# A stage's first weight block multiplied tile by tile, low weights first, from turned tiles that lie in PSUM banks of their own

## The chip, the cores and the metric

One Trainium2 chip, one of its cores. The metric is the device time of the program in microseconds, median of several executions. Engines by the names of the profile: PE (TensorE matmuls), PEld (its weight loads), DVE (VectorE), ACT (ScalarE), POOL (GpSimd), SP (SyncE, which issues the weight transfers).

## What is computed

Two transformer blocks, one behind the other, on 256 tokens with 1024 features, all in float32. The first has a mixer (gated MLP, forgetting attention, attention to a memory) and a feed-forward layer with squared ReLU; the second has two layers, each a half-weighted SwiGLU, an attention (sliding window in layer 0, latent in layer 1) and another SwiGLU. Every part begins with a normalisation of x:

```python
def rmsnorm(x, g):
    xf = x.astype(jnp.float32)
    y = xf * lax.rsqrt(jnp.mean(jnp.square(xf), axis=-1, keepdims=True) + RMS_EPS)
    return (y * g.astype(jnp.float32)).astype(x.dtype)
...
        h = rmsnorm(x, norm_pre_ffn[l])
        f = jnp.square(jax.nn.relu(h @ w_ff1[l])) @ w_ff2[l]
        x = x + rmsnorm(f, norm_post_ffn[l])
...
def swiglu(h, wg, wu, wd):
    return (jax.nn.silu(h @ wg) * (h @ wu)) @ wd
...
    for i in range(DEPTH_2):
        x = x + 0.5 * swiglu(rmsnorm_2(x, ffn_norm1[i]), ffn1_wg[i], ffn1_wu[i], ffn1_wd[i])
        h = rmsnorm_2(x, mix_norm[i])
```

## The kernel before

**Stages.** The program runs M1, F0, F1, MA, F2, F3, MB, F4: the mixer of the first block, its feed-forward layer (F0, "relu"), and then two layers of SwiGLU (F1, F3), attention (MA, MB) and SwiGLU (F2, F4). x lies in SBUF as two token tiles of 128 (`t`), 1024 features wide.

**Products.** Precision comes from pairs: every weight and every activation is held as an upper part rounded to fp32r (`w_hi`, `h_hi`) and a lower part that is left (`w_lo`, `h_lo`). A product is hi x hi, hi x lo and lo x hi. `h_both` holds both parts of h side by side, so `wide_features_out` (L282) takes hi weights against 512 columns (both parts, `of_hi`, L288) and lo weights against 256 (`of_lo`, L292); `sum_halves` (L317) adds the two halves of the bank. `tokens_out` has the tokens as stationary side and makes three products of 256 or fewer columns (L262 to L264).

**Weights.** A list of blocks (mostly 128 x 2048) is loaded by SP through a ring of six raw slots. For every block ScalarE rounds (`round_block`, L231) and VectorE subtracts (`split_block`, L238), into a ring of three; `hi_ready`, `lo_ready` and `block_used` count blocks.

**A turn.** Between two stages, x must be transposed and normalised. This happens nine times, n = 0 (the memory), 1, and 2 to 8, where n = 2 stands before F0, 3 before F1, 4 before MA, 5 before F2, 6 before F3, 7 before MB and 8 before F4. I call them turns. From n = 2 on:

- TensorE: `plain_tensor_turn` (L437) transposes 8 tiles of 128 features for each token tile, when `x_ready` says that the half of x is there. Feature tiles 2j and 2j+1 share a bank. `keep_busy` (L258) are filler products on constants, ahead, amid and behind the transposes by `TURN_IDLE`; two of them (four passes of the array) stand behind at every turn.
- ScalarE: `norm_scalar_round` (L504) scales the eight tiles with the gain and rounds them into `h_hi`, for each pair of tiles when the pair is transposed, and then takes the squares of the second token tile (L377), for the scale 1/rms.
- VectorE: `norm_vector_split` (L513) makes `h_lo`, for each pair when ScalarE has done the pair. Then it splits one weight block, in most turns makes two diagonal matrices of the scale (`row_vector_diag`), splits another block and copies the row of scales (`row_vector_copy`). At n = 7 it waits for the second scale before it splits the first of these blocks.
- GpSimd: `rsqrt_pool` (L388, L389) turns the sum of squares into the scale.
- TensorE again: the first block of the stage is called with `wait_h` and waits for `h_lo_ready` pair by pair. In the F stages it takes the first 128 output features with hi and lo in turn, then the second 128 with all hi and then all lo. Then `row_tensor` (L475) spreads the scales over the partitions, and the second block follows.

The scale is applied later, to the sums, so that products need not wait for it. In MA the first block (256 columns) is `a_in`, in MB it is the first of `b_in` (160 columns), both by `tokens_out`.

**What sets the order.** Each engine runs its own list, written out by hand, in order. Semaphores tie the lists together. No scheduler moves anything.

Of the kernel before, what the change touches and what calls it, by code (L numbers as in the profile page):

```python
# [6 lines left out]
F32 = mybir.dt.float32  # L7
F32R = mybir.dt.float32r
I32 = mybir.dt.int32
ALU = mybir.AluOpType  # L10
# [20 lines left out]
def build(nc, i, out):  # L31
# [80 lines left out]
    with ExitStack() as ctx:  # L112
# [143 lines left out]
        def keep_busy(bank, count):  # L256
            for _ in range(count):
                nc.tensor.matmul(ps[:, bank, 0:TOK], ident[:, :], tri[:, 0:TOK], start=True, stop=True, skip_group_check=True)  # L258
# [10 lines left out]
        def features_out(b, to, turn=0, wait_h=None, of=tokens):  # L269
# [12 lines left out]
        def wide_features_out(b, bank, turn=0, wait_h=None):  # L282
# [4 lines left out]
            def of_hi(f, k):  # L287
                nc.tensor.matmul(ps[:, bank + f, :], hi[:, k, f * P:(f + 1) * P], h_both[:, k, :, :].rearrange("p a b -> p (a b)"),  # L288
                                 start=k == 0, stop=False, skip_group_check=True)

            def of_lo(f, k):
                return nc.tensor.matmul(ps[:, bank + f, 0:TOK], lo[:, k, f * P:(f + 1) * P], h_both[:, k, 0, :],  # L292
                                        start=False, stop=k == KD - 1, skip_group_check=True)

            if wait_h is not None:
                nc.tensor.wait_ge(lo_ready, b + 1 + RAW * turn)
                for k in range(KD):
                    if k % 2 == 0:
                        nc.tensor.wait_ge(h_lo_ready, wait_h + k // 2 + 1)
                    of_hi(0, k)  # L300
                    of_lo(0, k)
# [4 lines left out]
            for k in range(KD):  # L306
                of_hi(1, k)
            if wait_h is None:
# [3 lines left out]
            for k in range(KD):  # L312
                last = of_lo(1, k)
# [6 lines left out]
        def tokens_out(b, to, turn=0, wait_h=None, h0=0, wait_k=None, half_done=None, before=None, half_count=1, of=tokens):  # L320
# [5 lines left out]
            for t in order:  # L326
                if before and t == order[1]:
                    before()
                for c in range(0, cols, 512):
                    w = min(512, cols - c)  # L330
                    for k in range(k_n):
                        if wait_h is not None and t == order[0] and c == 0 and k % 2 == 0:
                            nc.tensor.wait_ge(h_lo_ready, wait_h + k // 2 + 1)
# [8 lines left out]
        def tokens_half(b, half, bank, wait_h=None):  # L342
# [4 lines left out]
            for t in range(TT):  # L347
                for k in range(k_n):
                    h = k_n * half + k
                    if wait_h is not None and t == 0:  # L350
                        nc.tensor.wait_ge(h_lo_ready, wait_h + h // 2 + 1)
# [10 lines left out]
        def turn_bank(n):  # L362
            return 2 if n in (2, 5, 8) else 0
# [43 lines left out]
        def norm_vector_diag(n):  # L407
            for t in range(TT):
                c = 2 * n + t
                nc.vector.wait_ge(norm_rstd, c + 1)  # L410
                if t == 0:
                    if n:
                        nc.vector.wait_ge(h_psum, 4 * n)
# [4 lines left out]
        def norm_tensor_turn(n, source):  # L418
            for t in range(TT):
                nc.tensor.wait_ge(diag_ready, 2 * n + t + 1)  # L420
                for k in range(KD):
                    col = (k % 2) * TOK + t * P
# [1923 lines left out]
```

## Time and profile before

| | us |
|---|---|
| median of 3 runs | 1248.69 |
| lowest and highest | 1248.62, 1248.9 |
| span of the profiled execution, first to last instruction | 1246.7 |
| what lies around the span (median less span) | 2.0 |

| engine | busy us | share of the span |
|---|---|---|
| PE | 1219.2 | 98% |
| PEld (beside PE) | 1045.0 | 84% |
| DVE | 897.9 | 72% |
| ACT | 617.3 | 50% |
| POOL | 127.7 | 10% |

Read it so: TensorE has work nearly all the time, and the shares of the others are averages over stages. At a turn, though, a short chain runs through all engines, and there TensorE may wait, or be filled with products that nobody needs. Filler counts as busy in the first table. So the turns have to be read in the timeline, engine by engine, with the time at which each operation starts.

### The profile page before, as it was taken

The page shows a single profiled execution, that of the slowest core. Times are in us where ns is not written, and L with a number is a line of the kernel's source. Part 1 is how long each engine was busy: PE and PEld are TensorE (multiplying, and loading weights), DVE is VectorE, ACT ScalarE, POOL GpSimd, SP SyncE. Part 2 cuts the span into 40 slices and gives each one's busy share as a digit, 9 for nine tenths or more (in the row PEclk, how much of TensorE's full clock was granted, in tenths as well). Part 3 has the DMA queues.
Part 4 walks back from the last instruction along what each step waited for, and adds up shares of the span by engine and source line. Part 5 has one row for each costly group of instructions (what it writes and reads, how often), then busy time and mean ns, then how long its engine had stood idle before and what let it go on. Part 6 is the DMA issues. An engine that isn't in the chain of part 4 may idle for free.

```text
span 1246.7 us, 17409 instructions
## 1 busy us (share of the span) xinstructions
PE 1219.2 (98%) x6798; PEld 1045.0 (84%) x6798; DVE 897.9 (72%) x1088; ACT 617.3 (50%) x795; POOL 127.7 (10%) x169
## 2 busy tenths in 40 slices
PE   7999999999999999989999999999999989999998
PEld 7996788888888888967888888888888877888887
DVE  5976777667967777675877776877676775877675
ACT  6765444444643444685534444544434795534442
POOL 4420300000400000340000000100000430000000
PEclk9999999999999999999999999999999999999999
DMA  9882595556565656443555555656554414556530
GB/s 309 252 238 98 123 263 194 182 201 202 180 210 188 200 179 194 167 133 102 182 190 200 180 193 169 198 182 201 185 176 149 135 35 135 186 186 201 180 123 34
DMA packets 156039, 219.36 MB, mean 176 GB/s; under 512 B 6104, under 2 KB 134172, under 8 KB 155852
## 3 DMA queue, kind: packets, MB, share of 16 engines
q1 hardware_dynamic: 153612, 212.28, 52.8%
q0 software_dynamic: 2368, 6.26, 2.1%
q8 instruction: 40, 0.66, 0.2%
q14 instruction: 19, 0.16, 0.0%
HBM read 213.26 MB, written 5.27 MB: 175 GB/s over the span
## 4 chain that ended last, share of the span: by engine, by line
PE 90%; DVE 5%; ACT 3%; issue 1%; POOL 1%; DMA 0%; SPq 0%; DVEq 0%; ACTq 0%; POOLq 0%
PE ps L288 30%; PE ps L292 15%; PE ps L262 13%; PE ps L263 13%; PE ps L264 13%; PE ps L677 1%; PE ps L702 1%; PE ps L690 1%; ACT h_both L504 1%; DVE w_lo L238 1%; DVE arena L782 1%; ACT w_hi L231 0%; DMA raw<-in_w_mem_kv 0%; DVE h_both L513 0%; PE ps L449 0%
## 5 line engine op out<-in xcount | busy, mean ns | idle before, releaser
L231 ACT CAST w_hi<-raw 128x2048 fp32r<-128x2048 f32 (+3 forms) x198 | 375.5, 1899 | 399.2 <-PE ps L292 270.3
L238 DVE TENSOR_TENSOR w_lo<-raw,w_hi 128x2048 fp32r<-128x2048 f32 (+3 forms) x197 | 449.6, 2284 | 152.6 <-ACT w_hi L231 150.5
L288 PE MATMUL ps<-h_both,w_hi 128*128 128x512 f32 x1664 | 402.3, 391 | 1.4 <-DVE h_both L513 1.4
L288 PEld LDWEIGHTS ps<-h_both,w_hi 128*128 128x128 f32 x1664 | 308.8, 188 | 66.6 <-issue 3.2
L292 PEld LDWEIGHTS ps<-h_both,w_lo 128*128 128x128 f32 x1664 | 216.1, 191 | 8.1
L292 PE MATMUL ps<-h_both,w_lo 128*128 128x256 f32 x1664 | 222.2, 283 | 0.0
L262 PE MATMUL ps<-w_hi,act_hi 128*128 128x512 f32 x500 | 195.9, 392 | 1.1 <-DVE act_lo L1985 0.7
L263 PE MATMUL ps<-w_lo,act_hi 128*128 128x512 f32 x500 | 195.2, 390 | 0.0
L264 PE MATMUL ps<-w_hi,act_lo 128*128 128x512 f32 x500 | 194.5, 389 | 0.0
L317 DVE TENSOR_REDUCE arena<-ps 128x512 f32<-128x1024 f32 x104 | 127.3, 1224 | 81.4 <-PE ps L292 80.7
L262 PEld LDWEIGHTS ps<-w_hi,act_hi 128*128 128x128 f32 x500 | 94.1, 188 | 20.7 <-DVE act_lo L1985 1.1
L264 PEld LDWEIGHTS ps<-w_hi,act_lo 128*128 128x128 f32 x500 | 93.9, 188 | 20.0
L263 PEld LDWEIGHTS ps<-w_lo,act_hi 128*128 128x128 f32 x500 | 94.1, 188 | 17.2
L388 POOL TENSOR_SCALAR rstd<-sums 128x1 f32<-128x1 f32 (+1 forms) x22 | 20.8, 944 | 828.1 <-ACT scratch L377 648.9
L1178 ACT CAST act_hi<-act 128x512 fp32r<-128x512 f32 x60 | 37.4, 624 | 113.5 <-DVE act L1256 99.6
L262 PE MATMUL ps<-w_hi,h_both 128*128 128x512 f32 (+4 forms) x256 | 87.6, 342 | 1.4 <-DVE h_both L513 0.8
L263 PE MATMUL ps<-w_lo,h_both 128*128 128x512 f32 (+4 forms) x256 | 85.3, 333 | 0.0
L264 PE MATMUL ps<-w_hi,h_both 128*128 128x512 f32 (+4 forms) x256 | 85.1, 333 | 0.0
L262 PEld LDWEIGHTS ps<-w_hi,h_both 128*128 128x128 f32 x256 | 48.4, 189 | 8.9 <-issue 4.2
L264 PEld LDWEIGHTS ps<-w_hi,h_both 128*128 128x128 f32 x256 | 48.5, 189 | 4.0
L263 PEld LDWEIGHTS ps<-w_lo,h_both 128*128 128x128 f32 x256 | 48.5, 189 | 3.4
L484 DVE TENSOR_TENSOR arena<-arena,row 128x512 f32<-128x512 f32 x60 | 41.5, 692 | 2.1
(252 smaller groups left out, 1055.7 us busy)
## 6 DMA issues: line engine op xcount, KB each, us to landing
raw<-in_ffn_wg SPq DMA_DIRECT2D x44, 1024.0 KB, 5.3
raw<-in_ffn_wu SPq DMA_DIRECT2D x44, 1024.0 KB, 5.3
raw<-in_ffn_wd SPq DMA_DIRECT2D x44, 1024.0 KB, 4.9
raw<-in_w_ff SPq DMA_DIRECT2D x32, 1024.0 KB, 5.4
raw<-in_a_w_in SPq DMA_DIRECT2D x5, 1024.0 KB, 5.3
raw<-in_w_in SPq DMA_DIRECT2D x4, 1024.0 KB, 7.5
raw<-in_w_out SPq DMA_DIRECT2D x4, 1024.0 KB, 7.0
raw<-in_a_w_out SPq DMA_DIRECT2D x4, 1024.0 KB, 5.0
```

What stands on the lines that cost most here:

```text
L231: nc.scalar.copy(w_hi[:, place(b), 0:n], raw[:, b % RAW, 0:n]).then_inc(hi_ready, 1)
L238: nc.vector.tensor_tensor(w_lo[:, place(b), 0:n], raw[:, b % RAW, 0:n], w_hi[:, place(b), 0:n].bitcast(F32), ALU.subtract).then_inc(lo_rea ...
L262: nc.tensor.matmul(to, still[0], moving[0], start=start, stop=False, skip_group_check=True)
L263: nc.tensor.matmul(to, still[0], moving[1], start=False, stop=False, skip_group_check=True)
L264: return nc.tensor.matmul(to, still[1], moving[0], start=False, stop=stop, skip_group_check=True)
L288: nc.tensor.matmul(ps[:, bank + f, :], hi[:, k, f * P:(f + 1) * P], h_both[:, k, :, :].rearrange("p a b -> p (a b)"), start=k == 0, stop=F ...
L292: return nc.tensor.matmul(ps[:, bank + f, 0:TOK], lo[:, k, f * P:(f + 1) * P], h_both[:, k, 0, :], start=False, stop=k == KD - 1, skip_gro ...
L317: return nc.vector.tensor_reduce(to.rearrange("p (f t) -> p f t", f=2), ps[:, bank:bank + 2, :].rearrange("p f (h t) -> p f t h", h=2), AX ...
L388: pool_then(nc.gpsimd.tensor_scalar(to, sums_of, 1.0 / count, eps, ALU.mult, ALU.add))
L484: return nc.vector.tensor_tensor(to.rearrange("p (f t) -> p f t", f=2), source.rearrange("p (f t) -> p f t", f=2), row_of_both, ALU.mult)
L504: last = nc.scalar.activation(norm_home(n, k)[0], ps[:, turn_bank(n) + j, half * TOK:(half + 1) * TOK], ACT.Copy, scale=norm_gain(n, k))
L1178: nc.scalar.copy(act_hi[:, buf, :], act[:, buf, :]).then_inc(hidden_hi[st], 1)
```

## The change

1. **Banks.** For n = 2 to 8 the turned tiles 0 to 5 lie in six banks, one each, in the first half of the bank; tiles 6 and 7 lie in the second halves of the banks of tiles 4 and 5. Turns 0 and 1 stay as they were. Semaphores count tiles and not pairs. ScalarE takes a tile when it is turned (tiles 4 and 5 when 6 and 7 are turned too), and tiles 6 and 7 only when VectorE is through with 4 and 5. VectorE takes each tile when ScalarE has done it.
2. **Order of the first block.** For every feature tile k: lo weights x upper tokens for both halves of the output, as soon as `h_hi` of tile k is there; then hi weights x both parts for tile k-1, when `h_lo` of k-1 is there. In MA and MB a new function, `tokens_out_first`, does the same with the upper tokens as stationary side.
3. **Filler.** The two `keep_busy` products behind the transposes go, at all seven turns. Those ahead and amid keep their number and write to the second half of a bank.
4. **Row products.** `row_tensor` moves from behind the first block into the middle of the second (`amid`), between the hi products of its two halves.
5. **Bank moves that follow.** The first gate block of F1 and F3 goes to banks 6 and 7, the `a_in` blocks start at bank 6 (`a_bank`), the first two of MB at 6 and 5; two of the later transposes in MA swap banks and one waits for one more `a_squares`.

```diff
         def wide_features_out(b, bank, turn=0, wait_h=None, amid=None):
...
             if wait_h is not None:
+
                 nc.tensor.wait_ge(lo_ready, b + 1 + RAW * turn)
-                for k in range(KD):
-                    if k % 2 == 0:
-                        nc.tensor.wait_ge(h_lo_ready, wait_h + k // 2 + 1)
-                    of_hi(0, k)
-                    of_lo(0, k)
+                for k in range(KD + 1):
+                    if k < KD:
+                        nc.tensor.wait_ge(h_hi_ready, wait_h + k + 1)
+                        for f in range(2):
+                            of_lo(f, k)
+                    if k:
+                        nc.tensor.wait_ge(h_lo_ready, wait_h + k)
+                        for f in range(2):
+                            last = of_hi(f, k - 1)
...
-        def turn_bank(n):
-            return 2 if n in (2, 5, 8) else 0
+        def turned(n, k):
+
+            if n < 2:
+                bank, half = k // 2, k % 2
+            else:
+                bank, half = (2 if n in (2, 5, 8) else 0) + (k if k < 6 else k - 2), k // 6
+            return ps[:, bank, half * TOK:(half + 1) * TOK]
...
-        TURN_IDLE = {2: (0, 3, 2), 3: (1, 2, 2)}
+        TURN_IDLE = {2: (0, 3), 3: (1, 2)}
...
-            keep_busy(left, behind)
...
         def norm_scalar_round(n):
...
+            for k in range(KD):
+                nc.scalar.wait_ge(h_psum, 8 * n + (k + 2 - k % 2 if n < 2 else k + 3 if k in (4, 5) else k + 1))
+                if n >= 2 and k >= 6:
+                    nc.scalar.wait_ge(h_lo_ready, 8 * n + k - 1)
+                nc.scalar.activation(norm_home(n, k)[0], turned(n, k), ACT.Copy, scale=norm_gain(n, k)).then_inc(h_hi_ready, 1)
...
         def norm_vector_split(n):
...
+            for k in range(KD):
+                nc.vector.wait_ge(h_hi_ready, 8 * n + (k + 2 - k % 2 if n < 2 else k + 1))
...
         def swiglu_tensor(st, n, s, turn=0):
...
-            wide_features_out(b_gate(st, s), 0, turn=turn, wait_h=4 * n if s == 0 else None)
-            if s == 0:
-                row_tensor(n)
+            wide_features_out(b_gate(st, s), gate_bank(st, s), turn=turn, wait_h=8 * n if s == 0 else None)
...
-            wide_features_out(b_upper(st, s), 2, turn=turn)
+            wide_features_out(b_upper(st, s), 2, turn=turn, amid=(lambda: row_tensor(n)) if s == 0 else None)
```

The new function of MA and MB, with its main part:

```python
        def tokens_out_first(b, bank, wait_h):
...
            for k in range(KD + 1):
                if k < KD:
                    nc.tensor.wait_ge(h_hi_ready, wait_h + k + 1)
                    for t in range(TT):
                        still = h_hi[:, k, t * P:(t + 1) * P]
                        nc.tensor.matmul(to(t), still, hi[:, k, :], start=k == 0 and t == 0, stop=False, skip_group_check=True)
                        nc.tensor.matmul(to(t), still, lo[:, k, :], start=False, stop=False, skip_group_check=True)
                if k:
                    nc.tensor.wait_ge(h_lo_ready, wait_h + k)
                    for t in range(TT):
                        last = nc.tensor.matmul(to(t), h_lo[:, k - 1, t * P:(t + 1) * P], hi[:, k - 1, :],
                                                start=False, stop=k == KD, skip_group_check=True)
```

TensorE at turn 3, from the last transposes into the first block of F1, before the change (`ident,x` are transposes, `tri,ident` filler, `w_hi` and `w_lo` the halves of the weights):

```order
L449 MATMUL ps<-ident,x 128x128 x3
L258 MATMUL ps<-tri,ident 128x256 x2
L288 MATMUL ps<-h_both,w_hi 128x512 [waits h_lo_ready,lo_ready]
L292 MATMUL ps<-h_both,w_lo 128x256
L288 MATMUL ps<-h_both,w_hi 128x512
L292 MATMUL ps<-h_both,w_lo 128x256
L288 MATMUL ps<-h_both,w_hi 128x512 [waits h_lo_ready]
```

The same place with the change:

```order
L480 MATMUL ps<-ident,x 128x128 x3
L292 MATMUL ps<-h_both,w_lo 128x256 [waits h_hi_ready,lo_ready]
L292 MATMUL ps<-h_both,w_lo 128x256
L292 MATMUL ps<-h_both,w_lo 128x256 [waits h_hi_ready]
L292 MATMUL ps<-h_both,w_lo 128x256
L288 MATMUL ps<-h_both,w_hi 128x512 [waits h_lo_ready]
L288 MATMUL ps<-h_both,w_hi 128x512
L292 MATMUL ps<-h_both,w_lo 128x256 [waits h_hi_ready]
```

The filler is gone, four lo products stand ahead of the first hi product, and the first wait is for the upper part of one tile, not for the lower part of two.

ScalarE at turn 2, from x's first to its second tile of squares (L377), before the change:

```order
L504 ACTIVATE h_both<-ps,gain_col 128x256 [waits h_psum]
L504 ACTIVATE h_both<-ps,gain_col 128x256
L504 ACTIVATE h_both<-ps,gain_col 128x256 [waits h_psum]
L504 ACTIVATE h_both<-ps,gain_col 128x256
L377 ACTIVATE scratch,sums<-x 128x1024 [waits y_sumsq,sumsq_ready,x_ready]
```

The same place with the change (the squares are now L410):

```order
L534 ACTIVATE h_both<-ps,gain_col 128x256 [waits h_psum] x6
L534 ACTIVATE h_both<-ps,gain_col 128x256 [waits h_lo_ready,h_psum] x2
L410 ACTIVATE scratch,sums<-x 128x1024 [waits y_sumsq,sumsq_ready,x_ready]
```

The list is the same, but the last two tiles, and with them the squares, now stand behind VectorE (`h_lo_ready`).

## Rows read from the trace of the kernel before

**Rows 1.** The page: busy time and share of TensorE; the chain by engine.
```profile
PE 1219.2 (98%) x6798; PEld 1045.0 (84%) x6798; DVE 897.9 (72%) x1088; ACT 617.3 (50%) x795; POOL 127.7 (10%) x169
...
PE 90%; DVE 5%; ACT 3%; issue 1%; POOL 1%; DMA 0%; SPq 0%; DVEq 0%; ACTq 0%; POOLq 0%
```

**Rows 2.** Timeline of TensorE at turn 3: start us, us, engine, line, operation.
```profile
320.29 1.03 PE L258 MATMUL ps<-tri,ident 128*128 128x256 f32 x4
...
321.50 0.47 PE L288 MATMUL ps<-h_both,w_hi 128*128 128x512 f32 x1 [0.19 <-DVE h_both L513]
...
321.81 0.28 PE L292 MATMUL ps<-h_both,w_lo 128*128 128x256 f32 x1
...
324.57 2.01 PE L288 MATMUL ps<-h_both,w_hi 128*128 128x512 f32 x8
...
327.37 0.61 PE L475 MATMUL ps<-diag,tri 128*128 128x128 f32 x4
...
331.48 2.08 PE L292 MATMUL ps<-h_both,w_lo 128*128 128x256 f32 x16
...
333.39 3.82 PE L288 MATMUL ps<-h_both,w_hi 128*128 128x512 f32 x16
```

**Rows 3.** Timeline at turn 3 of ScalarE, VectorE and GpSimd.
```profile
319.61 3.05 ACT L504 ACTIVATE h_both<-ps,gain_col 128x256 fp32r<-128x256 f32 x8 [1.31 <-PE ps L449]
...
320.48 3.22 DVE L513 SCALAR_TENSOR_TENSOR h_both<-ps,gain_col,h_both 128x256 fp32r<-128x256 f32 x8 [0.74 <-ACT h_both L504]
...
323.78 2.18 POOL L388 TENSOR_SCALAR rstd<-sums 128x1 f32<-128x1 f32 x1 [3.63 <-ACT scratch L377]
...
329.54 1.22 DVE L317 TENSOR_REDUCE arena<-ps 128x512 f32<-128x1024 f32 x1
```

**Rows 4.** Timeline of TensorE at turn 6.
```profile
777.78 1.03 PE L258 MATMUL ps<-tri,ident 128*128 128x256 f32 x4
...
785.08 0.61 PE L475 MATMUL ps<-diag,tri 128*128 128x128 f32 x4
```

**Rows 5.** Timeline of TensorE and VectorE at turn 4.
```profile
506.35 1.03 PE L258 MATMUL ps<-tri,ident 128*128 128x256 f32 x4
...
509.91 4.48 DVE L238 TENSOR_TENSOR w_lo<-raw,w_hi 128x2048 fp32r<-128x2048 f32 x2
...
513.74 0.28 PE L262 MATMUL ps<-w_hi,h_both 128*128 128x256 f32 x1
```

**Rows 6.** Timeline at turn 2 of TensorE, VectorE and GpSimd.
```profile
139.91 2.28 DVE L238 TENSOR_TENSOR w_lo<-raw,w_hi 128x2048 fp32r<-128x2048 f32 x1
...
140.07 2.17 POOL L388 TENSOR_SCALAR rstd<-sums 128x1 f32<-128x1 f32 x1 [3.63 <-ACT scratch L377]
...
142.91 0.15 DVE L468 TENSOR_SCALAR y_scale<-rstd 128x1 f32<-128x1 f32 x1 [0.46 <-POOL rstd L389]
...
149.19 0.69 DVE L1182 TENSOR_TENSOR act_lo<-act,act_hi 128x512 fp32r<-128x512 f32 x1 [0.69 <-ACT act_hi L1178]
...
149.98 0.47 PE L262 MATMUL ps<-w_hi,act_hi 128*128 128x512 f32 x1
```

**Rows 7.** Timeline at turn 7 of TensorE, VectorE and GpSimd.
```profile
964.06 1.03 PE L258 MATMUL ps<-tri,ident 128*128 128x256 f32 x4
...
967.77 0.19 POOL L388 TENSOR_SCALAR rstd<-sums 128x1 f32<-128x1 f32 x1 [4.46 <-ACT scratch L377]
...
968.62 4.49 DVE L238 TENSOR_TENSOR w_lo<-raw,w_hi 128x2048 fp32r<-128x2048 f32 x2 [0.92 <-POOL rstd L389]
...
971.18 0.32 PE L262 MATMUL ps<-w_hi,h_both 128*128 128x256 f32 x1
```

**Rows 8.** Waits of TensorE: for whom, us in total, times, longest us.
```profile
PE ps L677 <- DVE small L782: 5.7, 9, 1.2
```

**Rows 9.** Groups of instructions: line, operation, count; busy us, mean ns; idle.
```profile
L423 PE MATMUL ps<-diag,arena 128*128 128x128 f32 x32 | 5.7, 359 | 0.0
...
L423 PE MATMUL ps<-diag,x 128*128 128x128 f32 x32 | 3.7, 275 | 0.0
```

More of the change, by code:

```diff
@@ L305, in wide_features_out @@
                     of_hi(0, k)
-            for k in range(KD):
-                of_hi(1, k)
-            if wait_h is None:
+                if amid:
+                    amid()
+                for k in range(KD):
+                    of_hi(1, k)
                 nc.tensor.wait_ge(lo_ready, b + 1 + RAW * turn)
@@ L311, in wide_features_out @@
                     of_lo(0, k)
-            for k in range(KD):
-                last = of_lo(1, k)
+                for k in range(KD):
+                    last = of_lo(1, k)
             last.then_inc(block_used, 1)
@@ L431, in x_halves @@
             return 4 * r + 2 * t + half + 1
-        TURN_IDLE = {2: (0, 3, 2), 3: (1, 2, 2)}
+        TURN_IDLE = {2: (0, 3), 3: (1, 2)}
         def plain_tensor_turn(n):
-            ahead, amid, behind = TURN_IDLE.get(n, (0, 0, 2))
-            left = y_bank(n - 2, 0) + 1
-            keep_busy(turn_bank(n) + 3, ahead)
+            ahead, amid = TURN_IDLE.get(n, (0, 0))
+            spare = 2 if n == 2 else 0
+            keep_busy(spare, ahead, TOK)
             for t in range(TT):
@@ L2070, in project @@
                     for half in halves_now:
-                        tokens_half(b + half, half, bank, wait_h=4 if p == 2 and half == 0 else None)
+                        tokens_half(b + half, half, bank, wait_h=8 if p == 2 and half == 0 else None)
                 elif features:
@@ L2202, in _ @@
                         tensor.wait_ge(a_squares, p - 3)
-                    tokens_out(first["a_in"] + p, lambda t, c, w: ps[:, 4 + p % 4, t * TOK + c:t * TOK + c + w],
-                               wait_h=16 if p == 0 else None, before=(lambda: scores_tensor(heads_a[0:2])) if p == 4 else None)
+                    if p == 0:
+                        tokens_out_first(first["a_in"], a_bank(0), 32)
+                        continue
+                    tokens_out(first["a_in"] + p, lambda t, c, w: ps[:, a_bank(p), t * TOK + c:t * TOK + c + w],
+                               before=(lambda: scores_tensor(heads_a[0:2])) if p == 4 else None)
                     if p >= 2:
@@ L2247, in turn_latent @@
                     last.then_inc(c_turned, 1)
-                tokens_out(first["b_in"], lambda t, c, w: ps[:, 4, t * TOK + c:t * TOK + c + w], wait_h=28)
+                tokens_out_first(first["b_in"], 6, 56)
                 b = first["b_in"] + 1
```

86 lines of the change are left out of this document (42 added, 44 removed).

## The prediction, made before the changed kernel ran

> **What bounds the kernel now.** The page's shares come first. TensorE is busy for 1219.2 of 1246.7 us and the chain that ended last is 90% PE [rows 1]: only what shortens TensorE's own line, or a hole in it, moves the end. The median of the runs, 1248.69, is the span and 2.0 us around it; I subtract from the span and add the 2.0 back.
>
> The change works at the seven turns n = 2 to 8, where a stage's x is transposed and its first weight block multiplied. I read TensorE's timeline at turn 3 [rows 2]. The last transpose is followed at 320.29 by the "behind" filler, the first product starts at 321.50, the second half's products run 324.57 to 327.37, and there the row products (L475) begin. From the end of the transposes to the end of the block it is 7.08 us. The work in it: the second half's eight hi products (512 columns) and eight lo products (256 columns) take 327.37 - 324.57 = 2.80 us, or 0.35 a pair, so 16 pairs make 5.6 us. A lo product alone takes (333.39 - 331.48) / 16 = 0.119 us, which leaves 0.231 for a hi product. So 1.47 us of the turn is filler, wait and pacing. The other engines show why [rows 3]: ScalarE rounds eight tiles in 3.05 us from 319.61 (0.36 us each), VectorE starts 0.87 later at 320.48, after two of them, and takes 3.22 (0.39 each). TensorE starts when VectorE's second tile is done, and then is held at VectorE's 0.39 us against its own 0.35 per tile.
>
> **The change, part by part.**
>
> *Order of the products, separate banks, filler gone.* No product is added or dropped. The new first block needs only the rounded upper tile to begin. ScalarE waits for one transpose, not two, so it starts about 0.1 earlier (one transpose cadence); its first tile is there about 0.5 later, near 320.05, before the transposes end at 320.29. VectorE now follows one tile behind ScalarE, not two: it starts near 320.0, its first lower tile is ready by about 320.65, with the 0.15 that a hand-over takes; TensorE asks for it after four lo products, at 320.29 + 0.48 = 320.77. From then TensorE uses 0.70 us a tile (two lo, two hi) against VectorE's 0.39, so it never waits again. It is its own bound: the block takes 5.6 us from 320.29 and ends at 325.9, against 327.37. Gain **1.47** at turn 3. The filler behind (four passes, 1.03 us) costs nothing now, since it covers the wait; once the wait is gone it would cost its whole 1.03, and its removal is part of this sum, not more. The fillers ahead and amid stay in number and only change bank: 0.
>
> Turns 5, 6 and 8 repeat the pattern. At turn 6 it is 777.78 to 785.08, or 7.30 [rows 4]; turns 5 and 8 have 7.19 and 7.17. There the transposes of both token tiles run together, so TensorE reaches the first lo product about 0.05 before its tile: 7.30 - 5.61 - 0.05 = **1.64** at turn 6, and about **1.57** each at 5 and 8.
>
> Turn 4 (a_in) has 48 products of 256 columns at 0.12: 5.76 us. Before, 506.35 to 513.74 is 7.39 [rows 5]. With 0.05 at the start: **1.58**. The next block then wants the lower part of its weights at 512.16. VectorE makes two splits of 2.24 from 509.91; moved 0.25 earlier (below), the first ends at 511.9. It is just met.
>
> *What is late next.* ScalarE's tiles 6 and 7 share a bank with 4 and 5 and wait until VectorE is through with them. ScalarE would start tile 6 at about +2.15 from its first, VectorE's tile 4 ends at 0.5 + 5 x 0.39 = +2.5: ScalarE ends 0.35 later than before, and with it the squares of x's second tile (L377). VectorE ends its eight tiles 0.25 earlier (0.5 earlier start, less what it waits for the late tiles 6 and 7). Two turns hang on these two numbers.
>
> Turn 2 (relu stage): TensorE's first second-product starts at 149.98, right behind the lower half of the hidden activations (149.19 + 0.69 = 149.88) [rows 6], so it already waits for VectorE there. Behind that lies one unbroken VectorE line from 139.91: split, POOL's rstd, diagonal, split, row, sum, scaling. In the new kernel TensorE comes 1.5 us early and stands. What counts is the VectorE line, and its only gap is the wait for POOL, released at 142.91. POOL's L388 starts at 140.07 and takes 2.17 us, ending with VectorE's split (139.91 + 2.28 = 142.19); at turn 7, with no split running, the same operation takes 0.19 [rows 6, 7]. So POOL ends with the split, which comes 0.25 earlier; squares 0.35 later still fall inside it. Gain **0.25**. The Trainium skill, "SBUF — State Buffer", section "SBUF: two separate sides", says that VectorE and GpSimd share a port pair as an exclusive lock held for the whole instruction; the trace agrees (2.17 against 0.19). If POOL did not stand, this turn's gain would be 0.25 and the 0.46 us of VectorE's wait, 0.7 in all.
>
> Turn 7 (b_in): the first block is 964.06 to 971.18 [rows 7]; its 48 products are narrower (160 columns), so they take at most turn 4's 5.76 us and, started at 964.06, would end by 969.8, at least 1.3 us sooner. But here VectorE waits for the second rstd before it splits the second block's weights: ScalarE's squares, POOL at 967.77, split 968.62 to 970.9. TensorE may enter the second block only then. With the squares 0.35 later the split ends near 971.25, against a start at 971.18 before: **-0.1**. The whole gain turns into a wait of 1.4 us or a little more.
>
> *Do turns 3, 5, 6, 8 keep theirs?* TensorE's next condition on VectorE is the sum of the first block: VectorE starts it at 329.54 and takes 1.22, TensorE needs it at 333.39 [rows 2, 3]. Slack 2.6, after the change 2.6 - 1.47 + 0.25 = 1.4. The row products move to the middle of the second block, where their diagonals are ready; in turn 3 they would otherwise be asked for at 325.9, before POOL has released them. They take the same 0.36 either way. Turns 3, 5, 6 and 8 keep the gain. After turn 4, ScalarE takes each a_in block out as TensorE ends it, so it comes earlier with TensorE, and the attention, whose waits (5.7 us for VectorE's L782 [rows 8]) lie among engines that all start earlier, shifts as a whole.
>
> *Bank moves* (gates of F1, F3 in banks 6 and 7, a_bank, b_in in 6; the stricter wait of the last a_in transpose): each waits on work that is over when it is asked for; 0. Waits that are met cost nothing: at 331.48 and 333.39 the cadence stays 0.119 and 0.23 [rows 2]. Turns 0 and 1 keep their order and banks: 0.
>
> Sum: 1.47 + 2 x 1.57 + 1.64 + 1.58 + 0.25 - 0.1 = 8.0 us. 1246.7 - 8.0 = 1238.7; with 2.0 around it, **1240.7**.
>
> **The rivals.**
> 1. VectorE's line binds in the swiglu stages as it does in turn 2. Then turns 3, 5, 6, 8 gain 0.25 each: 1.58 + 5 x 0.25 - 0.1 = 2.7, **1246.0**. It needs VectorE 1.4 us later than its rows say. Against it stands the slack above. 8 in 100.
> 2. The clock falls in the new holes (1.3 us at turn 2, 1.4 or more at turn 7, with no filler). The longest wait of the kind now is 1.2 us [rows 8], at a granted clock of 1.00. For a price, the kernel's first 32 turning products took 5.7 us against 3.7 for the next 32 [rows 9]: 2 us for each fall, both turns: **1244.7**. The Trainium skill, "TensorE: Matmul & The Clock Gate", section "What's actually happening", makes throttling the default that activity lifts; no run here shows a fall after so short a hole. 8 in 100.
> 3. Waits cost even when met: an unmet one makes the first product 0.31 instead of 0.23 (321.50 to its successor at 321.81 [rows 2]). 16 waits x 0.08 at five turns is 6.4 of the 8.0: **1247.1**, no change. The met waits above speak against it. 6 in 100.
> 4. Slower: squares decide everywhere. If POOL's rstd follows ScalarE's squares and not the split, and VectorE's line behind it binds at all turns, each turn loses the 0.35 by which tiles 6 and 7 delay the squares: 7 x 0.35 = 2.4, **1251.1**. It decides once rstd is later than the split's end and the slack of 1.4 is gone. At turn 3 POOL's L388 takes 2.18 us [rows 3], as at turn 2: it stands under a split there too, so the squares have room to come late. 4 in 100.
> 5. Turns 2 and 7 gain too, if the squares come early enough: up to 1.3 each, **1238.1**. 8 in 100.
>
> **How the numbers follow.** The forecast has 66 in 100. A range of 1238.0 to 1245.0 holds it with rivals 2 and 5, 82 in 100. A measurement of this kernel tells 0.2% from no change, 2.5 us: below 1246.2 lie the forecast and rivals 1, 2, 5: 0.90 faster; rival 3 0.06; rival 4 0.04.
>
> **What the changed profile would show.** At turns 3, 5, 6, 8 the lo products follow the transposes at once, and the second block starts 5.6 us after them. PE's idle grows at two places only: about 1.3 us before the first second-product of F0, 1.4 or more before b_in's second block. The squares (L377's successor) start 0.35 later after the first rounded tile. I am wrong if TensorE stands inside the new block, if its cadence in it is over 0.70 us a tile, or if new PE waits on gate_summed or the a_in weights appear.

## The result, and the profile after

| | before, us | after, us |
|---|---|---|
| median | 1248.76 (5 executions, 1248.62 to 1249.04) | 1241.65 (5 executions, 1241.56 to 1244.47) |
| ratio to before | 1 | 0.995, 95% interval 0.9939 to 0.9961 |
| span of the profiled execution | 1246.7 | 1242.1 |

The kernel is faster by 7.1 us. I had forecast 1240.7. But the five executions are not one group. Three lie at 1241.56 to 1241.65 with a granted TensorE clock of 1.000, two at 1244.45 and 1244.47 with 0.997. The profiled execution is one of the latter. That is a second finding beside the first, and it was one of the rivals. The median is the time of an undisturbed execution only because three of the five were undisturbed.

The page of the changed kernel: TensorE's busy time fell by 5.7 us, and the chain is TensorE for 92% of the span, where it was 90% [rows 1].

```profile
PE 1213.5 (98%) x6770; PEld 1042.9 (84%) x6770; DVE 897.5 (72%) x1088; ACT 616.6 (50%) x795; POOL 124.3 (10%) x169
...
PE 92%; DVE 4%; ACT 2%; issue 1%; DMA 0%; POOL 0%; SPq 0%; DVEq 0%; ACTq 0%; POOLq 0%
```

Turn 3 in TensorE's timeline (start us, us, engine, line, operation) answers [rows 2]:

```profile
320.59 1.32 PE L480 MATMUL ps<-ident,x 128*128 128x128 f32 x8 [0.47 <-DVE x L641]
321.66 0.72 PE L292 MATMUL ps<-h_both,w_lo 128*128 128x256 f32 x4
322.22 0.63 PE L288 MATMUL ps<-h_both,w_hi 128*128 128x512 f32 x2
322.69 0.40 PE L292 MATMUL ps<-h_both,w_lo 128*128 128x256 f32 x2
322.93 0.62 PE L288 MATMUL ps<-h_both,w_hi 128*128 128x512 f32 x2
...
326.41 2.91 PE L288 MATMUL ps<-h_both,w_hi 128*128 128x512 f32 x12
```

No wait is printed between the transposes and the end of the block. A tile's four products take 322.93 - 322.22 = 0.71 us, and the steps from tile to tile behind it are 0.69 or 0.70. Of the twelve hi products from 326.41 on, four still belong to this block and eight to the next.

Turn 2, rows of ScalarE, VectorE and TensorE (answers [rows 6]):

```profile
135.90 2.30 ACT L534 ACTIVATE h_both<-ps,gain_col 128x256 fp32r<-128x256 f32 x6 [1.08 <-PE ps L480]
...
138.86 0.84 ACT L534 ACTIVATE h_both<-ps,gain_col 128x256 fp32r<-128x256 f32 x2 [0.65 <-DVE h_both L540]
...
143.16 0.15 DVE L498 TENSOR_SCALAR y_scale<-rstd 128x1 f32<-128x1 f32 x1 [0.46 <-POOL rstd L422]
...
149.43 0.69 DVE L1211 TENSOR_TENSOR act_lo<-act,act_hi 128x512 fp32r<-128x512 f32 x1 [0.68 <-ACT act_hi L1207]
...
150.22 0.47 PE L262 MATMUL ps<-w_hi,act_hi 128*128 128x512 f32 x1 [1.76 <-issue]
...
152.04 0.63 PE L264 MATMUL ps<-w_hi,act_lo 128*128 128x512 f32 x1
...
154.41 0.40 PE L264 MATMUL ps<-w_hi,act_lo 128*128 128x512 f32 x1
```

Turn 7, rows of the same engines and of POOL (answers [rows 7]):

```profile
961.44 0.87 ACT L534 ACTIVATE h_both<-ps,gain_col 128x256 fp32r<-128x256 f32 x2 [0.35 <-DVE h_both L540]
...
963.43 0.19 POOL L421 TENSOR_SCALAR rstd<-sums 128x1 f32<-128x1 f32 x1 [4.83 <-ACT scratch L410]
...
964.29 4.49 DVE L238 TENSOR_TENSOR w_lo<-raw,w_hi 128x2048 fp32r<-128x2048 f32 x2 [1.46 <-POOL rstd L422]
...
966.63 0.58 PE L262 MATMUL ps<-w_hi,h_both 128*128 128x256 f32 x1 [1.67 <-DVE w_lo L238]
967.01 0.42 PE L263 MATMUL ps<-w_lo,h_both 128*128 128x256 f32 x1
...
970.11 0.28 PE L263 MATMUL ps<-w_lo,h_both 128*128 128x256 f32 x1
```

TensorE now stands for 1.76 us at turn 2 and 1.67 us at turn 7. At turn 2 the view names nobody for the wait (`issue`), but the hole ends just behind VectorE's `act_lo` (149.43 + 0.69 = 150.12). Behind the hole of turn 2 a matmul of 512 columns takes 0.63 us instead of 0.40 for some time (152.04 against 154.41), behind that of turn 7 one of 256 columns takes 0.42 instead of 0.28 (967.01 against 970.11). The windows behind the two holes show the granted clock (third number from the end, after the engines' busy times), first of the changed kernel:

```profile
150.00:154.00 4.00, 3.77 (x10) 3.04 (x11) 2.89 (x3) 1.20 (x1) 0.00 (x0) 0.59 1.04 178
966.00:970.00 4.00, 3.37 (x16) 3.37 (x17) 3.07 (x4) 3.06 (x9) 2.79 (x2) 0.57 0.55 167
```

and of the kernel before:

```profile
150.00:154.00 4.00, 4.00 (x18) 3.33 (x19) 3.00 (x2) 0.97 (x1) 0.00 (x0) 1.00 1.03 168
966.00:970.00 4.00, 4.00 (x36) 3.92 (x35) 3.08 (x6) 3.48 (x5) 0.74 (x2) 1.00 0.00 0
```

0.59 and 0.57 are mixtures of the two levels, 2.4 and 1.2 GHz. In the first window ten matmuls stand where eighteen stood.

To place the gain I took the start of the second token tile's first transpose at each turn from the timelines, and the stretches between them. e1 (below) is the changed kernel with both holes filled, an execution without a fall of the clock; lengths in us, gains against the kernel before.

| stretch | before | after (profiled) | e1 | gain forecast | gain in e1 |
|---|---|---|---|---|---|
| start to turn 2 | 135.42 | 135.54 | 135.65 | 0 | -0.23 |
| turn 2 to 3 | 183.72 | 185.05 | 183.80 | 0.25 | -0.08 |
| 3 to 4 | 186.34 | 184.85 | 184.85 | 1.47 | 1.49 |
| 4 to 5 | 85.14 | 83.53 | 83.50 | 1.58 | 1.64 |
| 5 to 6 | 186.29 | 184.75 | 184.77 | 1.57 | 1.52 |
| 6 to 7 | 186.28 | 184.76 | 184.75 | 1.64 | 1.53 |
| 7 to 8 | 94.67 | 96.37 | 94.88 | -0.1 | -0.21 |
| 8 to end | 188.80 | 187.28 | 187.30 | 1.57 | 1.50 |
| span | 1246.66 | 1242.12 | 1239.48 | 8.0 | 7.18 |

The five turns with a gain came in as priced. The two falls of the clock cost 185.05 - 183.80 = 1.25 us and 96.37 - 94.88 = 1.49 us.

### The profile page after: what moved, and what is told of

The parts are those of the page before. It is cut to its first block, busy times and chain, and to the rows that moved or that the text cites. A ratio compares the mean times of both kernels' runs of the same rounds, so it can differ in the third digit from the quotient of the medians.

```text
span 1242.1 us, 17367 instructions
## 1 busy us (share of the span) xinstructions
PE 1213.5 (98%) x6770; PEld 1042.9 (84%) x6770; DVE 897.5 (72%) x1088; ACT 616.6 (50%) x795; POOL 124.3 (10%) x169
## 4 chain that ended last, share of the span: by engine, by line
PE 92%; DVE 4%; ACT 2%; issue 1%; DMA 0%; POOL 0%; SPq 0%; DVEq 0%; ACTq 0%; POOLq 0%
PE ps L288 31%; PE ps L292 16%; PE ps L262 13%; PE ps L263 13%; PE ps L264 13%; PE ps L703 1%; PE ps L728 1%; PE ps L480 1%; PE ps L716 1%; DVE arena L808 1%; DMA raw<-in_w_mem_kv 0%; DVE w_lo L238 0%; PE ps L972 0%; PE ps L973 0%; PE ps L455 0%
## 5 line engine op out<-in xcount | busy, mean ns | idle before, releaser
L421 POOL TENSOR_SCALAR rstd<-sums 128x1 f32<-128x1 f32 (+1 forms) x22 | 17.3, 787 | 827.5 <-ACT scratch L410 647.8
L262 PE MATMUL ps<-w_hi,h_both 128*128 128x512 f32 (+3 forms) x224 | 79.0, 353 | 2.3 <-DVE w_lo L238 1.7
L263 PE MATMUL ps<-w_lo,h_both 128*128 128x512 f32 (+3 forms) x224 | 77.1, 344 | 0.0
L264 PE MATMUL ps<-w_hi,h_both 128*128 128x512 f32 (+3 forms) x224 | 76.8, 343 | 0.0
L262 PEld LDWEIGHTS ps<-w_hi,h_both 128*128 128x128 f32 x224 | 43.1, 192 | 9.0 <-issue 2.6
L264 PEld LDWEIGHTS ps<-w_hi,h_both 128*128 128x128 f32 x224 | 43.0, 192 | 4.0
L263 PEld LDWEIGHTS ps<-w_lo,h_both 128*128 128x128 f32 x224 | 43.1, 192 | 3.5
```

What stands on the lines that cost most here:

```text
L262: nc.tensor.matmul(to, still[0], moving[0], start=start, stop=False, skip_group_check=True)
L263: nc.tensor.matmul(to, still[0], moving[1], start=False, stop=False, skip_group_check=True)
L264: return nc.tensor.matmul(to, still[1], moving[0], start=False, stop=stop, skip_group_check=True)
L421: pool_then(nc.gpsimd.tensor_scalar(to, sums_of, 1.0 / count, eps, ALU.mult, ALU.add))
```

## The experiments

All were timed in five rounds beside the kernel before. e1 to e4 ran together, then e5 to e8 on another chip, then e9 with e10 on the chip of e1 to e4.

### e1: fill both holes

```diff
             if s == 1:
                 nc.tensor.wait_ge(row_ready, FEED[2] + 1)
+                keep_busy(7, 3)
...
                 tokens_out_first(first["b_in"], 6, 56)
+                keep_busy(7, 3)
```

> The changed kernel, with three filler products (about 1.5 us) put into each of the two holes that its trace shows: ahead of the first second-product of F0 (turn 2) and ahead of b_in's second block (turn 7). Nothing else is changed. Theory A: the executions of the changed kernel at 1244.5 are those in which the clock falls to its lower level after the two holes, those at 1241.6 the ones in which it does not; with the holes filled every execution is near 1241.6 and the granted clock is 1.000 in all, since the fillers end before what TensorE waits for is there. Rival B: the slow executions come from something else (for example weights that land late); then some executions stay at 1244.5. Rival C: the filler runs past the end of the hole and costs up to 0.3 us at each place: 1242.0 or so.

Measured: 1241.79 (1241.72 to 1241.84), granted clock 1.000 in all five. TensorE at the two places, and the window behind the first:

```profile
148.42 1.46 PE L258 MATMUL ps<-tri,ident 128*128 128x256 f32 x6
150.29 0.50 PE L262 MATMUL ps<-w_hi,act_hi 128*128 128x512 f32 x1 [0.41 <-DVE act_lo L1211]
...
963.63 1.50 PE L258 MATMUL ps<-tri,ident 128*128 128x256 f32 x6
965.47 0.39 PE L262 MATMUL ps<-w_hi,h_both 128*128 128x256 f32 x1 [0.34 <-DVE w_lo L238]
```

```profile
150.00:154.00 4.00, 3.71 (x16) 3.06 (x17) 2.89 (x3) 1.31 (x1) 0.00 (x0) 1.00 1.01 145
```

The filler ends 0.41 and 0.34 us before the data is there, so it costs nothing: with the hole of turn 2 open and no fall behind it (profile of e10, below) the stretch is 183.80 too, with that of turn 7 open (e2) it is 94.90 against 94.88. The clock stays at 2.4 GHz, and no execution lies near 1244.5. That fits theory A. Five executions alone wouldn't show it, since three of the five of the changed kernel had no fall either; the rows of the clock behind the holes speak for it, here and in e9.

### e2 and e10: fill one hole only

e2 has only the first of the two added lines of e1, e10 only the second.

> The changed kernel with filler in the hole of turn 2 only (ahead of the first second-product of F0), none at turn 7. Theory A: each hole makes its own fall of the clock, at a price of half of 2.9 us; executions lie at 1241.6 or, if the clock falls at turn 7, at 1243.0. Rival: one hole brings the fall at both places, then all are at 1241.6 or at 1244.5.

> The changed kernel with filler in the hole of turn 7 only, the hole of turn 2 (1.8 us) left open. Theory A: some executions 1.7 us above the rest, with the clock down from about 150.7 us on and at no other place of the two; the rest at 1241.8. Rival: only the hole of turn 7 matters, then all are at 1241.8.

Measured. e2: 1241.7, 1241.8, 1241.87 and 1241.97 at a clock of 1.000, 1243.6 at 0.999, 1245.08 at 0.997. e10: 1241.56, 1241.79, 1242.03 and 1242.03 at 1.000, 1242.91 at 0.999, 1243.72 at 0.998. Each kernel with one hole has slower executions, but not always. That the hole brings them isn't shown by these counts: beside e10 the kernel before had 3 of 11 executions below 1.000, beside e2 it had 1 of 18. The execution at 1245.08 is further off than one fall of 1.5 us explains. No slow execution of the two has a trace, so where their clock fell stays open. The profiled executions of both had no fall, behind open holes of 1.67 us (e2) and 1.76 us (e10).

### e3: the filler behind the transposes put back

```diff
+            keep_busy(BEHIND[n], 2, TOK)
+
+        BEHIND = {2: 0, 3: 6, 4: 7, 5: 0, 6: 6, 7: 7, 8: 0}
```

> The changed kernel with the two filler products behind the transposes put back at all seven turns (into a bank that is free there). Theory of the prediction: with the new order nothing covers them, so at turns 3, 4, 5, 6 and 8 each set costs its 0.9 to 1.0 us, and at turns 2 and 7 it only shortens the hole: 5 x 0.95 = 4.7 us above the undisturbed 1241.6, 1246.3. The holes of turns 2 and 7 are then 0.9 us shorter, and the clock stays up. Rival: the filler still lies beside a wait for the upper tiles and costs under 1 us in all: 1242.5.

Measured: 1245.44 (1245.27 to 1245.63), clock 1.000 in all six. Turn 3:

```profile
320.54 1.03 PE L258 MATMUL ps<-tri,ident 128*128 128x256 f32 x4
321.21 0.83 PE L292 MATMUL ps<-h_both,w_lo 128*128 128x256 f32 x4
321.88 0.62 PE L288 MATMUL ps<-h_both,w_hi 128*128 128x512 f32 x2
```

The stretches behind turns 3, 4, 5, 6 and 8 are longer than in e1 by 0.83, 0.73, 0.75, 0.68 and 0.74 us, together 3.7; the others are the same. So the filler is a cost once nothing lies beneath it. It is less than the 4.7 that I expected: the four passes cost their distance and not their length. The next product starts 0.67 us after the first of them (321.21 - 320.54), not 1.03, and the block's first product starts 0.62 to 0.76 us later than in e1. The holes of turns 2 and 7 are 0.93 us long here, not closed, and no execution had a fall.

### e4: the kernel before without that filler

```diff
-            keep_busy(left, behind)
```

> The kernel before with only the two filler products behind the transposes taken away, at all seven turns. Theory of the prediction: they cover a wait for VectorE's second tile, so their removal alone brings 0: 1248.7. Rival: they hold up the first product by the idle that the issue behind them takes (0.1 us each): 1248.0. Second rival: the holes of 1.2 us that they leave bring the clock down in some executions, 1.4 us each time.

Measured: 1249.04, ratio 1.0001 (0.9992 to 1.001). Eight of eleven executions lie at 1248.55 to 1249.14 with the clock at 1.000, three at 1250.46 to 1250.96 with 0.997 or 0.998. The profiled one is of the latter. TensorE at turn 3, and the window there:

```profile
321.62 0.49 PE L288 MATMUL ps<-h_both,w_hi 128*128 128x512 f32 x1 [1.05 <-DVE h_both L512]
...
322.12 0.63 PE L288 MATMUL ps<-h_both,w_hi 128*128 128x512 f32 x1
```

```profile
321.00:325.00 4.00, 3.38 (x11) 2.99 (x12) 4.00 (x9) 4.00 (x8) 1.12 (x1) 0.62 0.00 0
```

Under the old order the filler's time was free, as the prediction had it. Its removal alone brings 0 and leaves a hole at each of the seven turns, 1.05 to 1.28 us long. In this execution the clock fell behind one of the seven, that of turn 3 (1.05 us, one of the two shortest), and the stretch from turn 3 to 4 is 187.69 us instead of 186.34, 1.35 more. That the filler kept the clock up before the change is likely from this, but not shown: 3 of 11 executions against 1 of 18 of the kernel before beside it are too few to tell apart.

### e5: tiles 6 and 7 in the banks of 2 and 3

```diff
-                bank, half = (2 if n in (2, 5, 8) else 0) + (k if k < 6 else k - 2), k // 6
+                bank, half = (2 if n in (2, 5, 8) else 0) + (k if k < 6 else k - 4), k // 6
...
-                nc.scalar.wait_ge(h_psum, 8 * n + (k + 2 - k % 2 if n < 2 else k + 3 if k in (4, 5) else k + 1))
+                nc.scalar.wait_ge(h_psum, 8 * n + (k + 2 - k % 2 if n < 2 else k + 5 if k in (2, 3) else max(k + 1, 8 if k > 3 else 0)))
...
-                    nc.scalar.wait_ge(h_lo_ready, 8 * n + k - 1)
+                    nc.scalar.wait_ge(h_lo_ready, 8 * n + k - 3)
```

Both fillers of e1 are in it.

> The kernel of e1 (holes filled), with tiles 6 and 7 in the second halves of the banks of tiles 2 and 3 instead of 4 and 5. ScalarE then waits for VectorE's tiles 2 and 3, which are long done when it comes to 6 and 7. Theory: ScalarE's stop before tile 6 (2.97 us after the second token tile's first transpose, against 2.58 in the kernel before) is what delays the squares at turn 7 and VectorE's last tiles at turn 2. Without it ScalarE starts tile 6 at about 2.5, the squares at 3.3, VectorE is 0.4 earlier (0.6 at turn 2, where the stop was longer). Turn 7 gains 0.4, turn 2 0.6, the other turns nothing: 1240.8 against 1241.8. Rival: the split ahead of the rstd or POOL's wait under it decides, and nothing is gained: 1241.8.

Measured: 1240.71 (1240.39 to 1240.72), clock 1.000. ScalarE at turn 2, and VectorE at turn 7:

```profile
136.18 3.18 ACT L534 ACTIVATE h_both<-ps,gain_col 128x256 fp32r<-128x256 f32 x8 [1.08 <-PE ps L480]
```

```profile
962.28 4.50 DVE L238 TENSOR_TENSOR w_lo<-raw,w_hi 128x2048 fp32r<-128x2048 f32 x2 [1.27 <-POOL rstd L422]
```

The eight tiles are one run of 3.18 us again, where the changed kernel had six, a stop of 0.65 us and two. At turn 7 VectorE starts its splits 5.31 us after the second token tile's first transpose, where it was 5.81. The stretch from turn 2 to 3 is 183.29 (0.51 less than e1), that from 7 to 8 is 94.38 (0.50 less), all the others behind turn 2 are the same within 0.02 (turn 2 itself is reached 0.17 later). So the stop before tile 6, small as it is, reached the end of the kernel at exactly the two turns where the prediction had VectorE's line or the squares in charge.

### e6: at turn 7, split first and wait afterwards

```diff
+                split_block(late - 1)
                 if n == 7:
                     vector.wait_ge(norm_rstd, 2 * n + 2)
-                split_block(late - 1)
```

The filler of turn 2 is in it, that of turn 7 is not.

> The kernel of e2 (hole of turn 2 filled), and at turn 7 VectorE splits the weights of b_in's second block before it waits for the second rstd, not after. Theory: at turn 7 the new order's gain (1.6 us) is eaten by this wait alone; TensorE then enters the second block 0.2 to 0.3 us after the first instead of 1.8, POOL's operation stands under the split and the rstd comes 1.3 later, which ScalarE has room for: turn 7 to 8 is 1.5 shorter, 1240.3. Rival: the rest of MB (its rstds, its lower halves) waits for the later rstd, and the gain goes there: 1241.8 or above.

Measured: 1240.35 (four executions at 1240.25 to 1240.51, one of them with the clock at 0.999; one at 1242.42, also at 0.999). The last has no trace. In the profiled execution neither turn has a hole of more than 0.42 us, so slower executions come without these holes too. VectorE and POOL at turn 7:

```profile
961.49 2.28 DVE L238 TENSOR_TENSOR w_lo<-raw,w_hi 128x2048 fp32r<-128x2048 f32 x1
964.49 2.29 DVE L238 TENSOR_TENSOR w_lo<-raw,w_hi 128x2048 fp32r<-128x2048 f32 x1 [0.72 <-POOL rstd L422]
```

```profile
962.17 1.64 POOL L421 TENSOR_SCALAR rstd<-sums 128x1 f32<-128x1 f32 x1 [4.83 <-ACT scratch L410]
963.90 0.55 POOL L422 TENSOR_TENSOR rstd<-rstd,halves 128x1 f32<-128x1 f32 x1
```

The stretch from turn 7 to 8 is 93.55, 1.33 less than in e1: the turn's gain is there, and MB does not give it back. POOL's operation takes 1.64 us now, where it took 0.19 (963.43 in the changed kernel). It starts at 962.17, under the split, and ends with it (961.49 + 2.28 = 963.77). With squares that come at any time within the split, its end is the split's end.

### e7: the old order of the halves

```diff
-                for k in range(KD + 1):
-                    if k < KD:
-                        nc.tensor.wait_ge(h_hi_ready, wait_h + k + 1)
-                        for f in range(2):
-                            of_lo(f, k)
-                    if k:
-                        nc.tensor.wait_ge(h_lo_ready, wait_h + k)
-                        for f in range(2):
-                            last = of_hi(f, k - 1)
+                for k in range(KD):
+                    nc.tensor.wait_ge(h_lo_ready, wait_h + k + 1)
+                    of_lo(0, k)
+                    of_hi(0, k)
+                for k in range(KD):
+                    of_lo(1, k)
+                for k in range(KD):
+                    last = of_hi(1, k)
```

Both fillers of e1 are in it. Within each half the lo products now stand ahead of the hi products, which the kernel before had the other way round, and the wait is for one tile, not for two.

> The kernel of e1 with the F stages' first block in the old order of halves: half 0 with both weights tile by tile as the lower tile comes, then half 1 (MA and MB keep the new order; banks, semaphores per tile and the missing filler stay as in the changed kernel). Theory of the prediction: the order is worth about 1.0 us at each of turns 3, 5, 6, 8 (the block would start at the lower tile, 0.5 later, and be held to VectorE's 0.39 us a tile, 0.5 more), and nothing at turn 2: 1241.8 + 4 x 1.0 = 1245.8. The other 0.5 of each turn's 1.5 come from waiting for one tile instead of two. Rival: the separate banks and the semaphores per tile bring most of it: under 1243.

Measured: 1246.23 (1245.63 to 1246.63), clock 1.000. Turn 3:

```profile
321.35 0.35 PE L292 MATMUL ps<-h_both,w_lo 128*128 128x256 f32 x1 [0.19 <-DVE h_both L539]
321.55 0.39 PE L288 MATMUL ps<-h_both,w_hi 128*128 128x512 f32 x1
...
323.05 0.39 PE L288 MATMUL ps<-h_both,w_hi 128*128 128x512 f32 x1
...
323.44 0.40 PE L288 MATMUL ps<-h_both,w_hi 128*128 128x512 f32 x1
```

The block starts 1.50 us after the first transpose instead of 1.07, and its hi products then come at VectorE's 0.39 us (323.05 to 323.44). The stretches behind turns 3, 5, 6 and 8 are longer than in e1 by 0.94, 0.98, 1.00 and 0.97. Of the 1.5 us at such a turn, then, 1.0 is the order. The other 0.5 are what is left by subtraction: one tile waited for instead of two, and the filler gone, which no run separates.

Not expected were 0.42 us at turn 2, which I had priced at nothing. The trace has the reason:

```profile
145.45 0.60 PE L504 MATMUL ps<-diag,tri 128*128 128x128 f32 x4
...
146.09 0.42 DVE L509 COPY row<-ps 128x256 f32<-128x256 f32 x1 [0.31 <-PE ps L504]
```

TensorE is later with the first block, so the row products in the middle of the second (part 4 of the change) come at 145.45, where they came at 144.22 in e1. VectorE now waits 0.31 us for them, and it is VectorE's line that sets the time at this turn.

### e8: the three repairs together

> e2, e5 and e6 together: hole of turn 2 filled, tiles 6 and 7 in the banks of 2 and 3, the split first at turn 7. Theory: VectorE's split at turn 7 ends before TensorE has done the first block, so no hole is left there. Turn 2 gains 0.6, turn 7 up to 1.7: 1239.5. If MB waits for the later rstd: 1241.2.

Measured: 1239.46 (1239.3 to 1239.79), clock 1.000 in all five, ratio to the kernel before 0.9924 (0.991 to 0.9937). TensorE at turns 2 and 7:

```profile
148.28 1.46 PE L258 MATMUL ps<-tri,ident 128*128 128x256 f32 x6
149.66 0.50 PE L262 MATMUL ps<-w_hi,act_hi 128*128 128x512 f32 x1
...
962.51 0.61 PE L346 MATMUL ps<-w_hi,h_both 128*128 128x160 f32 x4
962.96 0.35 PE L262 MATMUL ps<-w_hi,h_both 128*128 128x256 f32 x1
```

At turn 7 the second block follows the first without a wait. The stretch from 7 to 8 is 93.24, 1.43 less than before the change; that from 2 to 3 is 183.27, 0.45 less. This is the fastest version here, and both new holes are gone. Older waits of TensorE stay in it as in every kernel here, one of 2.07 us near 13 us and one of 1.21 us near 102 us.

### e9: the changed kernel again

> The changed kernel as it is, for more executions beside the kernel before on one chip. Theory A (holes bring the clock down in some executions): again most executions at 1241.6 to 1241.9 with granted clock 1.000, and some of them 1.4 (0.999) or 2.9 us (0.997) above. Rival: the slow executions of the first measurement were chance as in the kernel before (1 of 23 there so far in these two sessions), then all lie at 1241.7.

Measured: 1243.25, 1243.3 and 1243.38 at a clock of 0.999, 1244.12 and 1244.51 at 0.997, 1247.22 at 0.995; not one execution at 1.000, where I had expected most at it. Ratio 0.9956 (0.9941 to 0.9971). Of the kernel before, three of eleven executions beside it had a clock below 1.000 as well (1251.02 to 1252.89), eight lay at 1248.7 to 1249.23.

The profiled execution (1244.12) has the two falls at the places where the first profile had them:

```profile
150.00:154.00 4.00, 3.88 (x11) 3.06 (x12) 2.88 (x3) 1.11 (x1) 0.00 (x0) 0.61 1.03 152
966.00:970.00 4.00, 3.47 (x16) 3.47 (x17) 3.07 (x4) 2.96 (x8) 2.79 (x2) 0.58 0.60 175
```

The stretches behind turns 2 and 7 are 185.06 and 96.39, against 183.80 and 94.88 in e1, and the others are as in e1. The execution at 1247.22 is 5.6 us above the undisturbed time, more than two falls cost, and it has no trace.

All executions, as they ran together; "low" are those with a clock below 1.000:

| ran together | kernel before | kernels with a new hole open | new holes filled, shortened or closed |
|---|---|---|---|
| the result | 0 of 5 low | changed kernel 2 of 5 | |
| e1 to e4 | 1 of 18 | e2 2 of 6, e4 3 of 11 | e1 0 of 5, e3 0 of 6 |
| e5 to e8 | 0 of 14 | | e5 0 of 5, e6 2 of 5, e7 0 of 10, e8 0 of 5 |
| e9 and e10 | 3 of 11 | changed kernel 6 of 6, e10 2 of 6 | |

The changed kernel, with both holes, is low in 8 of 11, the kernel before in 4 of 48, the kernels of the last column in 2 of 36. None of the last ran beside e9, when the kernel before had most of its low executions too. A clock of 0.999 is not always a slower execution: of the two of e6, one took 1240.25, as little as the rest. So the holes make falls more frequent; that filling them brings the falls back to the rate of the kernel before is what the counts suggest; that it rules them out isn't shown.

## Why the prediction was right, and where it was not

**The mechanism and its size: right.** The working of turn 3 (5.6 us of products, started at the end of the transposes) gave 1.47 and measured 1.49; turns 4, 5, 6 and 8 gave 1.58, 1.57, 1.64 and 1.57 and measured 1.64, 1.52, 1.53 and 1.50. e7 shows that the order is the larger part of it at turns 3, 5, 6 and 8: delay of the start and VectorE's pacing, 1.0 us of 1.5. Turn 4, and the remaining 0.5, no run takes apart. The slack of 1.4 us on VectorE's first sum was enough, since TensorE has no new wait in these stages. Rivals 1 and 4 are out, and so is rival 5: turns 2 and 7 gained nothing until e5 and e6.

**Filler free before, a cost after: right, over-priced.** e4 showed 0 before, e3 a cost after, of 0.68 to 0.83 us a turn instead of my 1.03. I had added the length of a pipelined group; its cost is the distance to the next start.

**Met waits cost nothing: right.** Four products a tile take 0.70 us, as worked out, with two waits among them. Rival 3 is out.

**Turn 7: right in kind.** The gain became a wait of 1.67 us. -0.21 measured against -0.1. e6 names the cause: with the split ahead of the wait, 1.33 us come back.

**Turn 2: wrong by 0.33.** The failed step is "VectorE ends its eight tiles 0.25 earlier". At turns 3 to 8 VectorE's last tile starts 0.17 earlier than before, but at turn 2 it starts 0.13 later (4.23 us after the transpose against 4.10), since ScalarE began tile 6 at 3.32 us instead of 2.64. At the other turns this was 2.97 to 3.02. The delay of the squares was mis-sized with it: 0.35 forecast, 0.43 at most turns, 0.70 at turn 2. e5 closes the stop and brings 0.5 at each of the two turns that hang on it. At turn 3 tile 6 starts 0.1 us after VectorE's fifth tile ends (2.92 and 3.02 us after the transpose), which is what it waits for; at turn 2 the fifth ends at 2.93 too, but tile 6 starts only at 3.32, as the sixth ends. Why, with the same code, stays open. That POOL's rstd ends with the split, so that late squares do no harm of their own, held: in the changed kernel VectorE still waits 0.46 for it (143.16), as in [rows 6].

**Start-up: 0.23 of the difference in e1.** Turn 2 is reached at 135.42 in the kernel before and at 135.44 to 135.82 in the others. The text there is not changed in its order, and I read nothing into it.

**The clock: right as a mechanism, wrong in its chance.** Rival 2 had 8 in 100. One fall or both came in 8 of 11 executions of the changed kernel. The median of e9 was 1243.75, nearer to the 1244.7 of the rival than to the forecast, and it was luck that the median of the first five executions was one without a fall. The step that failed is the evidence against the rival. I had read one row, a longest wait of 1.2 us at a clock of 1.00 [rows 8], as if a hole of that length were safe. It is one execution's row, and it isn't the longest wait. Apart from the start of the kernel, the same view has this longer one, which ends at 14.60 us, with a clock of 1.00 from 13 to 20 us:

```profile
PE ps L262 <- DVE w_lo L513: 1.9, 1, 1.9
```

A hole of this length stands in every kernel here (1.5 to 2.3 us near 13 us), and no profiled execution shows a fall behind it. So such a hole does not always bring the clock down, and one that once did not is no proof for the next: e4, with seven holes of 1.05 to 1.28 us, shows a fall behind one. The price was over-sized: 2 us for a fall, against 1.25, 1.49 and 1.35 (e4) measured. I took it from the first turning products, whose 5.7 and 3.7 us [rows 9] can't price the clock: it was granted at 1.00 from 6 to 13 us, where the slower ones lie.

The prediction had both holes, their places and nearly their lengths (1.3 and 1.4 or more, against 1.76 and 1.67). It did not draw the conclusion that a hole just made where filler was just removed should be filled, which costs nothing (e1).

## What to carry to other kernels

Order the first products of a stage by what its operands' producers finish first, and let every product that needs only the early half run ahead. When that shortens one engine's part, look at each place for the next thing it waits for: at two of seven turns the gain turned into a wait. A small edit off TensorE's path brought 0.5 us of it back at turn 2 (another bank), and at turn 7 1.3 us by one line moved ahead of a wait. Where the change leaves TensorE standing for about as long as the holes here (1.05 us and more), put filler into that hole, sized to end before the data comes, since it cost nothing in e1; and time such a kernel over many executions, with the granted clock beside each, since a median of five can fall on either side.

## What the runs showed of the hardware

- The fall of the clock after a short hole is a matter of chance for the single execution: the same kernel gave 1.000 in three of five executions in one session and in none of six in another. In all profiled falls (the changed kernel's two, e9's two, e4's one) TensorE had stood for 1.05 to 1.77 us just before. The matmuls behind take 0.63 us instead of 0.40 (512 columns) or about 0.41 instead of 0.28 (256 columns), with a granted clock of 0.57 to 0.62 in the window of 4 us. The length of the hole alone doesn't decide: six other holes of 1.05 to 1.28 us in e4, those of 1.67 us in e2 and 1.76 us in e10, and the one of 1.5 to 2.3 us near 13 us in all twelve profiles had no fall behind them.
- Slower executions at a lower clock come without the new holes too: 4 of 48 of the kernel before (1251.02 to 1252.89) and one of e6 (1242.42). None of these has a trace.
- The Trainium skill, "TensorE: Matmul & The Clock Gate", section "What's actually happening", has the throttled level as the default which activity lifts; these runs show that the clock can drop to that level right behind a hole of as little as 1.05 us (e4).
- GpSimd's operation on one column takes 0.19 us alone. Moved under a VectorE split by one line of code, the same operation went from 0.19 to 1.64 us and ended within 0.05 us of the split's end (e6). In the kernel before at turn 4 it started under the first of two splits that follow each other (509.91 to 514.39 [rows 5]) and ended only with the second:

```profile
510.06 4.38 POOL L388 TENSOR_SCALAR rstd<-sums 128x1 f32<-128x1 f32 x1 [4.46 <-ACT scratch L377]
```

- The Trainium skill, "SBUF — State Buffer", section "SBUF: two separate sides", states an exclusive lock on the port pair that VectorE and GpSimd share, held for the whole instruction of whichever starts first. The rows of e6 agree with it: the split started at 961.49, GpSimd's operation at 962.17, and that ended at 963.81, the split at 963.77.
